# The doubling levels of the DeltaNet chunks with 64 moving columns in place of 128

## The reference

```python
low = jnp.where(strict, jnp.einsum('bhncd,bhnsd->bhncs', kb, k) * gamma, 0.0)
rhs = jnp.concatenate([v * beta[..., None], kb * jnp.exp(gc)[..., None]], axis=-1)
sol = lax.linalg.triangular_solve(jnp.eye(c, dtype=low.dtype) + low, rhs,
                                  left_side=True, lower=True)
```

## Time and profile before

| | us |
|---|---|
| median of three runs | 2007.48 (2005.52 to 2009.92) |
| the profiled execution | 2007.11 |
| its span | 2005.3 |
| PE busy | 1866.1 (93%) |
| DVE busy | 1033.7 (52%) |
| ACT busy | 722.1 (36%) |
| POOL busy | 326.1 (16%) |
| mean granted clock | 0.959 |

### The profile page before, as it was taken

How to read it: one execution, slowest core, us unless ns; L and a number is a source line. 1 busy time by engine, 2 the same in 40 slices (tenths; PEclk the granted TensorE clock), 3 DMA queues, 4 the chain that set the end, 5 groups by cost and what they waited for, 6 DMA issues and landing times. The chain is left out here.

```text
span 2005.3 us, 37040 instructions
## 1 busy us (share of the span) xinstructions
PE 1866.1 (93%) x13666; PEld 1716.1 (86%) x13666; DVE 1033.7 (52%) x1723; ACT 722.1 (36%) x1258; POOL 326.1 (16%) x434
## 2 busy tenths in 40 slices
PE   7899988889999999999999999699889999999996
PEld 5899977778768899999999899455569999999996
DVE  1478244444343666666622633456634667668223
ACT  3233333333034533334522511454444433335221
POOL 0344433333000022222100000000000122222000
PEclk9799989999679999999999999999989999999998
DMA  4222310000132122222332123777832222222322
GB/s 160 74 73 84 96 43 0 0 0 8 63 126 74 54 82 84 84 84 83 101 89 89 56 81 123 252 264 255 269 106 74 63 84 82 77 81 82 95 84 78
DMA packets 78627, 188.44 MB, mean 94 GB/s; under 512 B 9202, under 2 KB 26994, under 8 KB 78178
## 3 DMA queue, kind: packets, MB, share of 16 engines
q1 hardware_dynamic: 78034, 185.26, 29.2%
q0 software_dynamic: 528, 2.32, 0.3%
HBM read 176.00 MB, written 11.55 MB: 94 GB/s over the span
## 5 line engine op out<-in xcount | busy, mean ns | idle before, releaser
L572 PE MATMUL PB<-parts,wparts 128*128 128x288 f32 x9312 | 1261.1, 297 | 27.4 <-DVE wparts L532 9.6
L572 PEld LDWEIGHTS PB<-parts,wparts 128*128 128x128 f32 x9312 | 1251.2, 190 | 33.2 <-DVE wparts L532 18.8
L522 ACT ACTIVATE wparts<-ring 128x1024 fp32r<-128x1024 f32 x198 | 210.1, 1061 | 644.4 <-PE PB L572 641.8
L532 DVE TENSOR_TENSOR wparts<-ring,wparts 128x1024 fp32r<-128x1024 f32 x172 | 210.6, 1226 | 293.2 <-ACT wparts L522 283.9
L890 POOL COPY cnew<-arena 128x2 f32 (+1 forms) x106 | 114.5, 1080 | 345.8 <-DVE arena L820 345.8
L832 DVE SCALAR_TENSOR_TENSOR arena<-arena,ffw 128x512 f32<-128x512 f32 x176 | 132.9, 755 | 19.2 <-DVE arena L833 12.8
L817 DVE TENSOR_TENSOR arena<-PB,rstd_in 128x288 f32<-128x288 f32 x88 | 40.2, 457 | 133.7 <-PE PB L572 133.7
L527 POOL TENSOR_TENSOR wparts<-ring,wparts 128x1024 fp32r<-128x1024 f32 x26 | 63.8, 2454 | 77.3 <-ACT wparts L522 77.2
L794 ACT ACTIVATE arena<-arena,ffw 128x512 f32<-128x512 f32 x88 | 63.9, 726 | 27.8 <-issue 15.9
L1289 POOL TENSOR_TENSOR arena<-arena,pconst 128x768 f32<-128x768 f32 (+1 forms) x31 | 53.8, 1735 | 118.2 <-DVE arena L1211 57.4
L865 DVE SCALAR_TENSOR_TENSOR arena<-arena,dnw 128x512 f32<-128x512 f32 x54 | 64.8, 1201 | 9.2 <-DVE arena L866 2.6
(11 more groups left out here) (265 smaller groups left out, 2088.0 us busy)
## 6 DMA issues: line engine op xcount, KB each, us to landing
ring<-in_w SPq DMA_DIRECT2D x206, 512.0 KB, 3.5
arena<-in_kpages SPq DMA_DIRECT2D x64, 256.0 KB, 5.1
arena<-in_vpages SPq DMA_DIRECT2D x64, 256.0 KB, 5.0
arena<-in_kpages SPq DMA_DIRECT2D x64, 128.0 KB, 2.3
arena<-in_vpages SPq DMA_DIRECT2D x64, 128.0 KB, 2.3
membuf<-in_state_dn SPq DMA_DIRECT2D x6, 512.0 KB, 3.2
o_dns_s<-membuf SPq DMA_DIRECT2D x6, 512.0 KB, 2.6
hT<-in_xT SPq DMA_DIRECT2D x1, 2304.0 KB
```

The lines of the kernel that those rows point to most:

```text
L522: nc.scalar.activation(wparts[:, 0, k, :], ring[:, k, :], ACT.Copy).then_inc(hi_ready, 1)
L532: nc.vector.tensor_tensor(wparts[:, 1, k, :], ring[:, k, :], wparts[:, 0, k, :].bitcast(F32), ALU.subtract).then_inc(lo_ready, 1)
L572: last = nc.tensor.matmul(dst(b), wparts[:, part, k, block * P:(block + 1) * P], x[:, row_, b * HALF:(b + 1) * HALF], start=start and part ...
```

## The change

In levels 1 and up the products x and xt change only half the columns of `Tm` and `TT`: with the columns in blocks of 2^l, x is zero outside the blocks with an even number, and xt outside those with an odd one. The change streams only these 64 columns (32 for the samples) as moving operand, read with a stride, lets them land packed in the first 64 columns of each head's place in PSUM, and subtracts them from the matching strided columns of `Tm` and `TT`. The weights of the matmuls, the number of instructions, all waits and the m product stay.

```diff
+        def part_of(a, l, upper):
+            if len(a.shape) == 2:
+                return a.rearrange("p (k two b) -> p k two b", two=2, b=2 ** l)[:, :, upper, :]
+            return a.rearrange("p h (k two b) -> p h k two b", two=2, b=2 ** l)[:, :, :, upper, :]
+        def packed(a, l):
+            return a.rearrange("p h (k b) -> p h k b", b=2 ** l)
...
-                            last = nc.tensor.matmul(bank(2 + g, T, T)[:, h - 3 * g, :], TT[0:T, h, 0:T], M1[0:T, h, 0:T],
-                                                    start=True, stop=True)
+                            last = nc.tensor.matmul(bank(2 + g, T, T // 2)[:, h - 3 * g, :], TT[0:T, h, 0:T],
+                                                    part_of(M1[0:T, h, 0:T], l, 0), start=True, stop=True)
...
-                        last = nc.tensor.matmul(bank(4 + g, T, T)[:, h - 3 * g, :], M1[0:T, h, 0:T], TT[0:T, h, 0:T],
-                                                start=True, stop=True)
+                        last = nc.tensor.matmul(bank(4 + g, T, T // 2)[:, h - 3 * g, :], M1[0:T, h, 0:T],
+                                                part_of(TT[0:T, h, 0:T], l, 1), start=True, stop=True)
...
-                        nc.vector.tensor_tensor(heads(Tm, g, T, T), heads(Tm, g, T, T), bank(2 + g, T, T),
+                        t_ = part_of(heads(Tm, g, T, T), l, 0)
+                        nc.vector.tensor_tensor(t_, t_, packed(bank(2 + g, T, T // 2), l),
                                                 ALU.subtract).then_inc(S_, mark(f"x{l}_{g}"))
...
-                    nc.vector.tensor_tensor(heads(TT, g, T, T), heads(TT, g, T, T), bank(4 + g, T, T),
+                    t_ = part_of(heads(TT, g, T, T), l, 1)
+                    nc.vector.tensor_tensor(t_, t_, packed(bank(4 + g, T, T // 2), l),
                                             ALU.subtract).then_inc(S_, mark(f"xt{l}_{g}"))
```

## The result

The changed kernel takes 2016.7 us, median of nine runs (2009.1 to 2019.9), beside 2006.2 for the kernel before in nine (2001.3 to 2009.9). The ratio is 1.0043, 95% interval 1.0026 to 1.0059: slower by 0.4%, which is 10.5 us by the medians and 8.6 by the ratio. Its profiled execution took 2017.6 us with a span of 2015.8, 10.5 us more than that of before. The mean granted clock fell from 0.959 to 0.953.

A forecast was written before the change was run, and what follows sets the result against it. PE's record cadence (112 ns at 2.4 GHz, 213 at 1.2) was taken to bound the levels, with its clock mattering as much. 7.3 - 1.0 - 0.1 = +6.2 us on 2007.1 gave 2013.3 us, range 2004 to 2022.

The forecast's parts named there:

- The cadence: PE's x and xt matmuls: 112 ns a record with full weights however few columns stream, so halving takes 0 us off.
- The end of the record: Last matmul record of a group: 222 ns with 64 columns, 275 with 128, so VectorE may start 53 ns sooner.
- The subtractions: VectorE's L1231 and L1235: 0.20 us shorter each; with the sooner start 0.24 us per chunk, -1.0 us over four chunks.
- The clock: PE in level 1 of three chunks: clock rises only after level 2's m group, 2.4 us a chunk, +7.3 us.
- The sample chunk: Sample chunk's levels: cadence by weights again, last subtraction at most 0.1 us shorter, -0.1 us.
- The sum: Whole kernel: 7.3 - 1.0 - 0.1 = +6.2 us, giving 2013.3 us.
- Nothing moves: Rival: PE's clock follows idle time alone, so only -1.1 us remains, 2006.0 us; chance 0.22.
- Clock low throughout: Rival: PE's clock stays low through the chunks' levels, +73 us over four chunks, about 2080 us; chance 0.06.
- Moving columns set the cadence: Rival: x and xt records of 64 moving columns cost 58 ns, -16.6 us in all, about 1990 us; chance 0.08.
- slow strides: Rival: strided f32 moving operands take four times the time a column, costing 53 us, 2060 us; chance 0.04.

The follow-up runs named there:

- Narrow weights: Changed kernel, but x and xt load only the first 64 weight columns and VectorE subtracts those 64 rows alone, half of each update left out: 1986.2 us, ratio 0.9911.
- VectorE's half: Changed kernel, but PE streams all 128 columns in x and xt; VectorE still subtracts only the 64 changed columns, strided: 2005.2 us, ratio 0.9994.
- the filling: Eight extra 128x256 matmuls per prompt chunk in PE's waits ahead of the levels; kernel before 1997.0 and 2000.7 us, changed kernel 1994.6 and 1995.9 us.
- the filled kernel before: Kernel before the change plus eight extra 128x256 matmuls per prompt chunk ahead of the levels: 1997.0 us (ratio 0.9954), on a second chip 2000.7 us (0.9968).
- the kernel without strides: Changed kernel, but x, xt and the subtractions take the first 64 columns in one piece, so the inverse is not computed: 2013.4 us, ratio 1.0034.

## Why the prediction was right, point by point

- **The cadence, 0 us.** Right: 4.27 us a level before and after, 0.67 us for six records. Which row to take was the choice of this prediction: L1026 (58 ns) and L1115 (113 ns) had both few moving columns, and only the second had the change's weights. Narrow weights gave 58 ns.
- **The end of the record, 53 ns sooner.** Right in what it did, for a reason that the row didn't give. L1071's records still have a median of 275 ns, and the 222 ns of L1026 came with its narrow weights too. But the step behind the last xt shows the time: 1.46 us with 128 columns and VectorE's half, 1.41 with 64.
- **The subtractions.** 351 ns forecast, 354 measured; 0.24 us at the end of the levels, 0.25 measured (0.20 and 0.05, as forecast).
- **The clock, +7.3 us.** That the loss is PE's late rise behind the fall is shown by the experiments with levels 1 and 2 wide, with these alone halved, and with the filling. The size: I had three chunks with one level of delay each, 2.4 us apiece. The profile has two chunks delayed, one by a level (+3.05 us) and one by two (+6.23, just over the bound of 2.4 + 3.6), and the fourth gained, since it rose 3.4 us after its m group began (458.97 to 462.37), where it had been 5.2 before. Four chunks together: forecast 7.3 - 1.0 = 6.3, measured -1.10 + 3.05 + 6.23 - 1.12 = 7.1. That the two sums agree so well is in part luck: the larger delay of one chunk made up for the chunk that had none, and the first chunk's gain came mostly from a stretch of the clock that the change doesn't touch.
- **The sample chunk, -0.1 us.** Wrong: +2.5. I had seen that its levels never raise the clock, and took that as nothing to lose. But the low stretch ran on through the first head's matmuls (506.74 to 534.05), where before it ended at 515.85. And what I had read as the levels' stretch (502.20 to 515.85) holds more than them: they end at 509.11, and the rise came behind the matmuls after them. Whether the change caused the longer stretch isn't shown: the filled kernel before has 27.3 us here too in its second profile, and the kernels with levels 1 and 2 halved and with narrow weights, which halve the sample chunk's columns as well, have 13.7.
- **The sum.** 2013.3 forecast, 2017.6 in the profiled execution and 2016.7 in the median, inside 2004 to 2022. The profile rose by 10.5 us and not 6.2; of the missing 4.3 us, 2.6 are the sample chunk's term, 0.8 the prompt chunks' and 1.0 what lies outside the stage.
- **The rivals.** *Nothing moves*: refuted by the low stretches and by a ratio whose interval lies above 1. The rule of the Trainium skill that it went with ("TensorE: Matmul & The Clock Gate", section "HAM oscillation — how this bites in real kernels") names half of the matter: the gaps ahead of the levels do cause the falls, as the filling shows, but the loss came from matmuls without a gap between groups. *Clock low throughout*: refuted; the rises came by level 3 at the latest, and 64-column levels reached at 2.4 GHz stayed there. *Moving columns set the cadence* and *slow strides*: refuted by the level's 4.27 us and by the kernel without strides.

## What to carry to other kernels

Before moving columns are saved in a stream of small f32 matmuls, look for a row with the same weights and few moving columns: if its cadence is the same, the weights are the bound and only narrower weights help. A saving that leaves PE's records as far apart but half empty can cost clock where the clock has just fallen (here 10 us of 2006); look at what PE did in each stretch before a rise. And the cheapest gain here was neither: eight dummy matmuls in PE's waits ahead of the levels took the four chunks to 2.4 GHz from 264.5 us on and the changed kernel to 0.9946 and 0.9944 of the kernel before, in two comparisons.

## What the runs showed of the hardware that was not expected

- Records of 64 moving columns behind a load of 64 weight columns brought the clock up as early as full ones (6.8 us low in all four chunks), and behind a load of 128 didn't in two chunks of four (13.7 and 20.5), with the same number of columns streamed. It is one profile of each kernel.
- The runs of the changed kernel spread over 10.8 us, the three of the kernel before that I started from over 4.4 (8.7 in all nine). That isn't the change's doing: in the comparisons on three chips the kernel before spreads over 12.4, 19.0 and 11.3 us (33, 29 and 16 runs), so three runs had shown its scatter as far too small. The changed kernel's runs of 2009.1 and 2019.9 us have mean granted clocks of 0.956 and 0.950, so the spread goes with the clock; that it is a different mix of the low stretches (6.8, 13.7, 20.5) from run to run is argued and not shown, as only one execution of each kernel has its windows recorded.
- A matmul record's length in the trace goes by its weights too: with 64 moving columns its median is 275 ns behind 128 weight columns (L1071 of the changed kernel) and 222 behind 64 (the same line with narrow weights).
